# Scores issued before the turns, and a start that loads the activations ahead of the weights

## The reference

```python
def swiglu(x, w_gate, w_up, w_down):
    return (jax.nn.silu(x @ w_gate) * (x @ w_up)) @ w_down

# first block, per head (and per 128 queries)
s = jnp.einsum('bhgqd,bhkd->bhgqk', qb, kb) * scale     # scores
s = s + rel_bias(table, qpos, kpos)                     # bias from a table
p = softmax(where(mask, s, NEG))                        # probabilities
o = jnp.einsum('bhgqk,bhkd->bhgqd', p, vb)              # values

# second block, layer 0: dilated attention of 16 heads, layer 1: retention
```

## Time and profile before

| | us |
|---|---|
| median of 3 runs | 2851.09 |
| lowest, highest | 2848.41, 2851.96 |
| the profiled execution, its own time | 2854.93 |
| its span in the trace | 2853.1 |
| PE busy in it | 2778.7 (97%) |
| DVE, ACT, POOL busy | 1836.1, 1360.9, 103.9 |

### The profile page before, as it was taken

One profiled execution on the slowest core, in us unless ns is written; L12 is line 12 of the kernel. 1 busy time (PEld: TensorE's weight loads), 2 busy tenths in 40 slices (PEclk: granted clock), 3 DMA queues, 4 the chain that ended last, 5 costly groups with the idle time before them and its releaser, 6 DMA issues.

```text
span 2853.1 us, 41544 instructions
## 1 busy us (share of the span) xinstructions
PE 2778.7 (97%) x16646; PEld 2413.1 (85%) x16646; DVE 1836.1 (64%) x2800; ACT 1360.9 (48%) x1946; POOL 103.9 (4%) x135
## 2 busy tenths in 40 slices
PE   7999999999999999999999999998999998999998
PEld 6888988888888988888878889996888888988787
DVE  5666566566766656756676665554667666655666
ACT  4554444355455444435445544444545454453444
POOL 1000000000000000001011001110000000000000
PEclk9999999999999999999999999999999999999999
DMA  6454333445455543346445545453444454434443
GB/s 243 180 200 167 142 144 140 174 159 188 175 189 185 194 172 129 140 155 230 178 180 194 183 175 170 154 171 122 178 183 173 181 195 159 164 146 155 171 182 125
DMA packets 49044, 488.43 MB, mean 171 GB/s; under 512 B 6480, under 2 KB 6576, under 8 KB 10520
## 3 DMA queue, kind: packets, MB, share of 16 engines
q1 hardware_dynamic: 43192, 470.44, 44.8%
q0 software_dynamic: 5728, 16.25, 2.0%
HBM read 485.47 MB, written 1.19 MB: 171 GB/s over the span
## 4 chain that ended last, share of the span: by engine, by line
PE 88%; DVE 6%; ACT 3%; issue 1%; DMA 1%; POOL 0%; DVEq 0%; ACTq 0%; POOLq 0%
PE ps L855 68%; PE ps L915 15%; DVE ring_lo L1852 2%; ACT ring_hi L1496 1%; PE ps L1129 1%; PE ps L871 1%; PE ps L1333 1%; DMA norm_g<-norm_gT_dram 1%; DVE ring_lo L1865 1%; PE ps L1348 1%; PE ps L1240 0%; ACT ring_hi L1547 0%; DVE xn L1981 0%; DVE ring_lo L1908 0%; DVE h L1963 0%
## 5 line engine op out<-in xcount | busy, mean ns | idle before, releaser
L855 PE MATMUL ps<-uT,ring_hi 128*128 128x512 f32 (+1 forms) x5536 | 1519.8, 346 | 10.3 <-DVE qkT L2011 9.3
L855 PE MATMUL ps<-uT,ring_lo 128*128 128x256 f32 x4176 | 1177.7, 282 | 0.0
L855 PEld LDWEIGHTS ps<-uT,ring_hi 128*128 128x128 f32 x5536 | 958.7, 191 | 160.2 <-issue 18.0
L855 PEld LDWEIGHTS ps<-uT,ring_lo 128*128 128x128 f32 x4176 | 795.8, 191 | 6.2
L1945 DVE TENSOR_TENSOR ring_lo<-ring,ring_hi 128x2048 fp32r<-128x2048 f32 x160 | 366.9, 2293 | 221.0 <-ACT ring_hi L1547 221.0
L1852 DVE TENSOR_TENSOR ring_lo<-ring,ring_hi 128x3072 fp32r<-128x3072 f32 (+1 forms) x110 | 330.6, 3006 | 177.3 <-ACT ring_hi L1496 177.2
L1496 ACT ACTIVATE ring_hi<-ring 128x3072 fp32r<-128x3072 f32 (+1 forms) x110 | 273.5, 2487 | 300.9 <-PE ps L855 280.5
L1547 ACT ACTIVATE ring_hi<-ring 128x2048 fp32r<-128x2048 f32 x167 | 317.4, 1901 | 0.0
L915 PE MATMUL ps<-ring_hi,hid_hi 128*128 128x512 f32 x704 | 276.7, 393 | 0.0
L915 PE MATMUL ps<-ring_lo,hid_hi 128*128 128x512 f32 x704 | 275.9, 392 | 0.0
L915 PE MATMUL ps<-ring_hi,hid_lo 128*128 128x512 f32 x704 | 273.9, 389 | 0.0
(11 more groups left out here) (301 smaller groups left out, 2619.8 us busy)
## 6 DMA issues: line engine op xcount, KB each, us to landing
ring<-stream_dram SPq DMA_DIRECT2D x299, 1536.0 KB, 6.3
mlaT_all<-bias_vectors POOLq DMA_DIRECT2D x32, 96.0 KB, 2.8
bias<-gains_dram POOLq DMA_DIRECT2D x5, 512.0 KB, 7.5
yR<-bias_vectors POOLq DMA_DIRECT2D x1, 2048.0 KB, 11.1
mlaT_all<-bias_vectors POOLq DMA_DIRECT2D x32, 64.0 KB, 2.8
row<-ret_const_dram POOLq DMA_DIRECT2D x1, 1280.0 KB, 5.7
h<-x_rows_dram POOLq DMA_DIRECT2D x2, 512.0 KB, 11.8
yR<-gains_dram POOLq DMA_DIRECT2D x2, 512.0 KB, 9.8
```

Of the source, the lines that this page charges most:

```text
L855: m = pe.matmul(out_, lhsT, rhs, start=start, stop=stop, **kw)
```

## The change

Four things are changed.

1. In `attention` and in `dilated` the scores of a step stand ahead of the turn.
2. SP issues the table and the picks first, without the wait on DVE's memset, then `h`, `cst` and `norm_g`, which POOL issued before. POOL's six parameter transfers stand behind its first root.
3. Slots 0 and 1 are loaded in pieces: gate columns of slot 0, up columns of slot 0, front of slot 1, then the two backs.
4. ACT and DVE split the gate columns of slot 0 after four of the eight blocks of `uT`, the up columns after the other four, and the front of slot 1 after the squares. PE starts the gate half of slot 0 when the gate's low part is there (`gate_0_lo`).

```diff
@@ sync engine
-            load(stream[0, :, :], 0)
-            sp.wait_ge(table_masked, 1)
             sp.dma_start(table_sb[0:32, 0:20], table_1).then_inc(picks_in, 16)
             for n in range(2):
                 sp.dma_start(picks_sb[0:33, 512 * n:512 * n + 512], pick_1[:, 512 * n:512 * n + 512]).then_inc(picks_in, 16)
-            for s in range(1, NS):
+            loads = [(h[:, 0, :], x_rows[:, 0, :]), (h[:, 1, :], x_rows[:, 1, :]), (cst[:, :], consts),
+                     (norm_g[:, :, :, :], norm_gT)]
+            for dst, src in loads:
+                sp.dma_start(dst, src).then_inc(h_in, 16)
+            sp.dma_start(ring[:, 0, 0:D], stream[0, :, 0:D]).then_inc(gate_0_in, 16)
+            sp.dma_start(ring[:, 0, D:2 * D], stream[0, :, D:2 * D]).then_inc(up_0_in, 16)
+            sp.dma_start(ring[:, 1, 0:2 * D], stream[1, :, 0:2 * D]).then_inc(front_1_in, 16)
+            for s in range(2):
+                sp.dma_start(ring[:, s, 2 * D:3 * D], stream[s, :, 2 * D:3 * D]).then_inc(weights_in[s], 16)
+            for s in range(2, NS):
                 load(stream[s, :, :], s)
@@ tensor engine
                 def gate_up(c, t, i=None, first=False, end=False):
-                    split_weights(c, i)
+                    if c:
+                        split_weights(c, i)
                     for part in range(2):
+                        if c == 0 and part == 0:
+                            pe.wait_ge(gate_0_lo, 1)
+                        elif c == 0:
+                            split_weights(c)
...
             def attention(l):
                 for t in range(STEPS):
+                    if t < PAIRS:
+                        scores(l, t)
                     if 1 <= t <= PAIRS:
                         turn(l, t)
-                    if t < PAIRS:
-                        scores(l, t)
...
                 for s in range(NS2 + 1):
+                    if s < NS2:
+                        dilated_scores(s)
                     if s:
                         dilated_turn(s - 1)
-                    if s < NS2:
-                        dilated_scores(s)
@@ scalar engine
                     act.activation(dst, src, ACT.Copy, scale=gain[:, k:k + 1]).then_inc(uT_act_ready, 1)
+                    if p == 0 and k == 3:
+                        act.wait_ge(gate_0_in, 16)
+                        act.activation(high(0)[:, 0:D], ring[:, 0, 0:D], ACT.Copy).then_inc(gate_0_hi, 1)
+                if p == 0:
+                    act.wait_ge(up_0_in, 16)
+                    act.activation(high(0)[:, D:2 * D], ring[:, 0, D:2 * D], ACT.Copy).then_inc(hi_ready, 1)
                 act.activation(xn[:, 0, :], h[:, 0, :], ACT.Square, accum_out=h_sq[:, 0:1]).then_inc(h_squared, 1)
+                if p == 0:
+                    act.wait_ge(front_1_in, 16)
+                    act.activation(high(1)[:, 0:2 * D], ring[:, 1, 0:2 * D], ACT.Copy).then_inc(hi_ready, 1)
...
+                    if c < 2:
+                        act.wait_ge(weights_in[c], 16)
...
-            for c in range(2):
-                take_high(c)
@@ vector engine
+                    if p == 0 and k == 3:
+                        dve.wait_ge(gate_0_hi, 1)
+                        dve.tensor_tensor(ring_lo[:, 0, 0:D], ring[:, 0, 0:D], high(0)[:, 0:D].bitcast(F32),
+                                          ALU.subtract).then_inc(gate_0_lo, 1)
+                if p == 0:
+                    dve.wait_ge(hi_ready, 1)
+                    dve.tensor_tensor(ring_lo[:, 0, D:2 * D], ring[:, 0, D:2 * D], high(0)[:, D:2 * D].bitcast(F32),
+                                      ALU.subtract).then_inc(lo_ready, 1)
...
-            for c in range(2):
-                take_low(c)
             for l in range(DEPTH):
                 c = layer_slot(l) + C_FFN
-                norm(3 * l, norm_g[:, l, 0, :], late=layer_slot(l) + 1 if l else None)
+                norm(3 * l, norm_g[:, l, 0, :], late=layer_slot(l) + 1)
@@ gpsimd engine
-            loads = [(h[:, 0, :], x_rows[:, 0, :]), (h[:, 1, :], x_rows[:, 1, :]), (cst[:, :], consts),
-                     (norm_g[:, :, :, :], norm_gT)]
-            for dst, src in loads:
-                pool.dma_start(dst, src).then_inc(h_in, 16)
...
+            pool.wait_ge(filled, 2)
+            root(0)
             for dst, src in loads:
                 pool.dma_start(dst, src).then_inc(params_in, 16)
-            pool.wait_ge(filled, 2)
-            root(0)
```

More of the change, by code:

```diff
@@ L327, in build @@
         h_in = sem("h_in")
+        gate_0_in = sem("gate_0_in")
+        up_0_in = sem("up_0_in")
+        front_1_in = sem("front_1_in")
+        gate_0_hi = sem("gate_0_hi")
+        gate_0_lo = sem("gate_0_lo")
         part_ready = sem("part_ready")
@@ L809, in _ @@
                 sp.dma_start(picks_sb[0:33, 512 * n:512 * n + 512], pick_1[:, 512 * n:512 * n + 512]).then_inc(picks_in, 16)
-            for s in range(1, NS):
+            loads = [(h[:, 0, :], x_rows[:, 0, :]), (h[:, 1, :], x_rows[:, 1, :]), (cst[:, :], consts),
+                     (norm_g[:, :, :, :], norm_gT)]
+            assert len(loads) == H_DMAS
+            for dst, src in loads:
[6 more added lines that the diff above has]
+            for s in range(2, NS):
                 load(stream[s, :, :], s)
@@ L2574, in output_roots @@
                                        ALU.pow).then_inc(ry_ready, 1)
-            loads = [(h[:, 0, :], x_rows[:, 0, :]), (h[:, 1, :], x_rows[:, 1, :]), (cst[:, :], consts),
-                     (norm_g[:, :, :, :], norm_gT)]
-            assert len(loads) == H_DMAS
-            for dst, src in loads:
-                pool.dma_start(dst, src).then_inc(h_in, 16)
             loads = [(mla_g[:, :, :], mla_gT), (flip, flip_dram), (sink[:, :, :], sinks.partition_broadcast(P)),
```

## The result

| | before | after |
|---|---|---|
| median of 4 runs each, same chip (us) | 2850.67 | 2828.66 |
| lowest, highest | 2848.41, 2851.96 | 2826.78, 2829.89 |
| span of the profiled execution | 2853.1 | 2828.0 |

The ratio is 0.9923, 95% interval 0.9906 to 0.9940: 22 us faster. Forecast were 2837.7 and a range down to 2833.5, so the direction was right and the gain was underestimated by 9 us. A later measurement of the same changed kernel gave 2827.4 against 2851.9, ratio 0.9916 [0.9902, 0.993].

A forecast was written before the change was run, and what follows sets the result against it. PE was taken as the bound, 88% of the span, so time is gained only where it idles. Start 7.1, first attention 0.8, dilated waits 2.0 and dilated end 3.5 sum to 13.4 us: 2851.09 to 2837.7, range 2833.5 to 2844.

The forecast's parts named there:

- Scores ahead of the turn, first attention: First attention: the reordering gains only PE's four short printed waits, 0.8 us, bounds 0 and 0.8; later turns cost nothing.
- the four waits of 0.2: First attention: PE waits, two behind DVE's scaling and two behind ACT's copy of the differential heads, all removed, 0.8 us.
- six dilated waits: Even dilated steps 2 to 12: PE's 0.33 us waits for a DVE copy vanish through an earlier signal, 2.0 us.
- the start: Kernel start: gate half of slot 0 begins 8.6 us earlier, less 1.5 for slow products, a gain of 7.1 us.
- H: Moment at which the transposes of `h` start: 8.0 us, bounds 7.0 and 12.6, in place of 19.79.
- the table load: Start: ACT's table load loses its cover, stands behind the first transposes and costs 1.28 us.
- the slow pairs: Start: PE's products are slow after idling, costing 1.5 us more than before, between 0 and 2.8.
- The end of the dilated attention: From step 14 on: earlier split and scores(15) ahead of turn(14) bring the output projection 3.5 us earlier, bounds 1.0 and 5.0.
- R1: Start: activations land no sooner than a transfer of theirs did, 12.6; sum 8.8 us, median 2842.3; chance 0.14.
- R2: End of the dilated attention gives only the shift, 1.0 us; sum 10.9, median 2840.2; chance 0.12.
- R3: Steps 8 to 20, both layers: merges wait for later turns, 21 us; kernel 8.5 slower, 2859.6; chance 0.04.
- The two signs: Prediction wrong if the start gives under 4 us, or new PE waits elsewhere total over a microsecond.

The follow-up runs named there:

- e9: Changed kernel plus a small early ACT activation that loads the table, and the postponed ring_used raise on the first product of the dilated values: 2826.11 us, ratio 0.9913.
- e1: Kernel before with scores ahead of the turn in `attention` alone: 2846.32 against 2851.04 us, ratio 0.9981.
- e3: Changed kernel with both attentions back in the old order, so only the start is new: 2843.03 us against 2851.04 for the kernel before, ratio 0.9973.
- e7: Changed kernel with slots 0 and 1 each loaded whole in one transfer again: 2828.51 us, ratio 0.9919 to the kernel before.
- e8: Changed kernel with `h`, `cst` and `norm_g` issued on POOL's queue again, beside SP's weights: 2831.41 us, ratio 0.9933 to the kernel before.
- e6: Changed kernel plus a small ACT activation ahead of everything, so ACT's table loads early: 2828.03 us against 2850.24 for the kernel before, ratio 0.9919.
- e2: Kernel before with scores ahead of the turn in `dilated` alone: 2840.93 against 2851.04 us, ratio 0.9967.
- e10: e9 plus throwaway products where PE idles at the start, five before the transposes and two before the first product with uT: 2826.67 us, ratio 0.9911.
- e4: Changed kernel with scores and turn cut and interleaved in dilated steps 1 to 13, same instructions: 2833.29 us, ratio 0.9937 to the kernel before.

## Why the prediction was wrong

**What failed** is one sentence of the step "Scores ahead of the turn, first attention": "PE does not wait in them, so nothing is gained but the four waits of 0.2". It priced a reordering of PE's products at nothing because none was added and no wait was printed. The swap takes one change of size out of each 64-row step. The first attention gained 5.15 us where I had 0.8 (bounds 0 to 0.8), and the dilated one 2.5 us by the sizes, where I had nothing. Of the four small waits only half went, worth 0.5 of the 5.15.

**The second error** is a term mis-sized: six dilated waits at the printed 0.33, 2.0 us, bounds 0 and 2.0. They were worth 0.56 each, 3.4. The idle time in brackets is a gap between rows whose ends are modelled; the distance of the starts of the same instruction in successive steps is what the step costs. My upper bound was the printed wait. So both errors lay beyond the range: its low end had 17.4 us, with 0.8 and 2.0 for terms that came to 5.15 and 5.8.

**The terms added up**: forecast 7.1 + 0.8 + 2.0 + 3.5 = 13.4; measured 7.9 + 5.15 + 5.8 + 3.4 = 22.3. The missing 9 us are 4.35 in the first attention, 2.5 and 1.4 in the dilated steps (the sizes, and the waits beyond what was printed), and 0.8 of the start.

**What held.** H at 8.0 (8.22), the table load behind the first transposes (9.42, 1.28 us), the first product at 14.5 (14.54), and that the first pairs are slow were right. How much the slow pairs cost was not: I had 1.5 us more than before, and it was 0.7, which is the 0.8 by which slot 1 came before 24. In e9, with no slow pair, it is 7.37 us from slot 0's first product to slot 1's; it was 8.03 before and is 8.71 in the changed kernel. The end of the dilated attention was right in its sum, with scores(15) ahead of turn(14) and both at the lower clock. That it hit 3.5 so closely is in part luck of the clock. The same distance was 20.1, 19.4 and 19.4 us in the old order with the old signal (before, e1, e3), and 16.7, 16.7, 16.0, 15.9, 15.4 and 15.1 in the new one (the changed kernel twice, e7, e8, e6, e2), so that other pairs of executions give anything from 2.7 to 5.0.

**The rivals.** R1 (H = 12.6) did not happen in the changed kernel; with the activations on POOL's queue it did, at 12.18. R2 (the end gives only 1.0) fell, it gave 3.4. R3 (the later turns are paid) fell: no wait for a gate or a merge's addition is printed in the first attention (there is a gap of 0.14 us at 500.17), and the attention became shorter. The two signs by which the prediction was to be called wrong, a start under 4 us and new waits of over a microsecond, did not come either: like the sum, they looked at waits alone.

**What stays open.** Why a change of size costs 0.18 to 0.2 us, and whether the three kinds of change cost the same (the rows show pauses from 0.11 to 0.25). Whether it is the size or the place: in the dilated attention the 64-row and 64-column products use the two halves of the array in turn, and no run keeps to one. Why `norm_g` landed so late in the kernel before is open too, and so is what decides whether the end of the dilated attention falls to the lower clock: of nine profiled executions with the new order there six had such a stretch, of differing place and length, and three (e2, e9, e10) had none.

## What to carry to other kernels

Where PE is busy over 95% of the time, read PE's rows for the size of the stationary operand and count its changes per step: an order that puts equal sizes side by side, or small ones side by side, takes about 0.2 us a change out of a stream in which no wait is printed. Price a wait by the distance of the starts over one period, not by the idle figure, and let no upper bound rest on that figure. A first instruction whose cost was hidden under a wait (here the table load) loses its cover when the wait is shortened: give it one that waits for nothing.

## What the runs showed of the hardware

- A change between 128\*128, 64\*128 and 128\*64 costs PE 0.18 us (e4, two more a step: 0.35) to 0.20 us (one less a step); between 96\*128 and 128\*128 it costs nothing that the rows show (e1).
- 1.4 MB in seven transfers at the head of SP's queue landed 7.4 us after issue (8.1 to 9.0 from the span's start over the executions); the same activations on POOL's queue beside the weights landed at 12.18.
- The length of the idle time before the first products didn't tell their clock alone. After 3.00 us idle (changed kernel) five pairs ran slowly, at a granted clock of 0.52, 0.63 for a high product that takes 0.40 at full speed. After 2.65 and 2.64 us the first pair was slow already in two executions (the changed kernel again; e3, eight pairs) and at full speed in two others (e7, e8), where the clock fell within the next pairs. After 1.43 us (e6, e9) and 0.27 (e10) no pair was slow.
